# Output projections ahead of the feed-forward layers: VectorE's row chunks interleaved, five of eight squares added by accumulating DMA inside SBUF

## The reference, cut to what matters

```python
def first_block(x, ...):
    for layer in range(DEPTH):                 # DEPTH = 2
        h = _rmsnorm(x, norm_mix_g[layer])
        mix = ...                              # layer 0: gated recurrence, layer 1: stick-breaking attention;
                                               # both end in y @ w_out, 1024 x 1024
        x = x + mix
        h = _rmsnorm(x, norm_ffn_g[layer])     # x * rsqrt(mean(x*x) + eps) * g
        x = x + _swiglu(h, ffn_w_gate[layer], ffn_w_up[layer], ffn_w_down[layer])   # inner width 2816
    return _rmsnorm(x, final_g)
# a second block with three kinds of attention follows; the change leaves it alone
```

## Time and profile before

| | |
|---|---|
| median of 3 runs | 1893.66 us (1890.73 to 1895.09) |
| the profiled execution's own time | 1895.13 us |
| its span | 1893.5 us |
| TensorE busy | 1859.5 us, 98% of the span |
| VectorE busy | 1282.3 us, 68% |
| ScalarE busy | 943.5 us, 50% |
| GpSimd busy | 233.2 us, 12% |
| granted TensorE clock, mean | 0.995 |

### The profile page before, as it was taken

One profiled execution on the slowest core, in us unless ns is written; L12 is line 12 of the kernel. 1 busy time (PEld: TensorE's weight loads), 2 busy tenths in 40 slices (PEclk: granted clock), 3 DMA queues, 4 the chain that ended last, 5 costly groups with the idle time before them and its releaser, 6 DMA issues.

```text
span 1893.5 us, 30168 instructions
## 1 busy us (share of the span) xinstructions
PE 1859.5 (98%) x10662; PEld 1556.0 (82%) x10662; DVE 1282.3 (68%) x2220; ACT 943.5 (50%) x1573; POOL 233.2 (12%) x322
## 2 busy tenths in 40 slices
PE   9999899999999999999999999999999999999998
PEld 7787799889988777689988998776777887777777
DVE  7687888548756666778745876576676565656553
ACT  6477576325544444556623554355655344445442
POOL 3111011001000000011101100000002054432000
PEclk9999999999999999999999999999999999999999
DMA  7334577257432122167535742212313233323221
GB/s 252 106 101 123 139 182 180 101 135 184 133 104 78 56 66 66 56 167 194 134 132 141 195 122 86 68 45 62 95 56 92 83 95 80 90 79 91 76 97 66
DMA packets 79219, 208.64 MB, mean 110 GB/s; under 512 B 10208, under 2 KB 18528, under 8 KB 79120
## 3 DMA queue, kind: packets, MB, share of 16 engines
q1 hardware_dynamic: 60080, 174.16, 28.6%
q0 software_dynamic: 19040, 33.20, 10.2%
HBM read 203.12 MB, written 4.21 MB: 109 GB/s over the span
## 4 chain that ended last, share of the span: by engine, by line
PE 86%; DVE 6%; DMA 3%; ACT 3%; issue 2%; DVEq 0%; SPq 0%; ACTq 0%; POOL 0%
PE ps L645 16%; PE ps L647 15%; PE ps L646 15%; PE ps L731 4%; PE ps L732 4%; PE ps L733 4%; PE ps L933 3%; PE tr L899 3%; PE sc L731 3%; PE sc L733 3%; PE sc L732 3%; DMA Wr<-in_w 2%; PE sc L856 2%; PE sc L645 1%; PE sc L646 1%
## 5 line engine op out<-in xcount | busy, mean ns | idle before, releaser
L645 PE MATMUL ps<-Hl,Wh 128*128 128x512 f32 x784 | 329.2, 420 | 0.0
L1343 ACT ACTIVATE Wh<-Wr 128x1024 fp32r<-128x1024 f32 (+2 forms) x172 | 195.6, 1139 | 253.7 <-PE ps L647 228.3
L647 PE MATMUL ps<-Hh,Wh 128*128 128x512 f32 x784 | 307.6, 392 | 0.0
L646 PE MATMUL ps<-Hh,Wl 128*128 128x512 f32 x784 | 307.0, 392 | 0.0
L1907 DVE TENSOR_TENSOR Wl<-Wr,Wh 128x1024 fp32r<-128x1024 f32 (+2 forms) x172 | 231.1, 1344 | 103.0 <-ACT Wh L1343 101.6
L645 PE MATMUL ps<-Yl,Wh 128*128 128x512 f32 (+1 forms) x648 | 253.3, 391 | 11.5 <-DVE Wl L1907 5.6
L646 PE MATMUL ps<-Yh,Wl 128*128 128x512 f32 (+1 forms) x648 | 249.6, 385 | 0.0
L647 PE MATMUL ps<-Yh,Wh 128*128 128x512 f32 (+1 forms) x648 | 249.3, 385 | 0.0
L645 PEld LDWEIGHTS ps<-Hl,Wh 128*128 128x128 f32 x784 | 147.7, 188 | 40.3 <-issue 11.1
L647 PEld LDWEIGHTS ps<-Hh,Wh 128*128 128x128 f32 x784 | 147.6, 188 | 33.2
L646 PEld LDWEIGHTS ps<-Hh,Wl 128*128 128x128 f32 x784 | 148.2, 189 | 25.8 <-issue 0.5
(11 more groups left out here) (404 smaller groups left out, 4149.7 us busy)
## 6 DMA issues: line engine op xcount, KB each, us to landing
Wr<-in_w SPq DMA_DIRECT2D x162, 512.0 KB, 3.6
Wr<-in_w SPq DMA_DIRECT2D x32, 768.0 KB, 4.2
scr<-in_w SPq DMA_DIRECT2D x66, 256.0 KB, 4.6
Wr<-in_w SPq DMA_DIRECT2D x66, 256.0 KB, 4.6
scr<-in_w SPq DMA_DIRECT2D x22, 512.0 KB, 5.7
scr<-in_w POOLq DMA_DIRECT2D x44, 256.0 KB, 7.4
Wr<-in_w POOLq DMA_DIRECT2D x44, 256.0 KB, 4.2
Wr<-in_w SPq DMA_DIRECT2D x16, 640.0 KB, 3.8
```

The source lines that it names most:

```text
L645: pe.matmul(bank[:, 0:n], hi, rl[:, k, :], start=(k == 0), stop=False)
L646: pe.matmul(bank[:, 0:n], lo, rh[:, k, :], start=False, stop=False)
L647: return pe.matmul(bank[:, 0:n], hi, rh[:, k, :], start=False, stop=(k == kc - 1))
L1343: act.activation(place(Wh, slot, kc), place(Wr, slot, kc), ACT.Copy).then_inc(w_hi, 1)
```

## The change

At both places the output units get functions of their own, `rows_out`, on ScalarE and VectorE.

- **VectorE's order.** The splits of units 5, 6 and 7 move ahead: between `even_quarters` and `even_lo` of chunk 2 and chunk 4, and between `odd_quarters` and `odd_lo` of chunk 3. The subtraction for `El` (now `rest_lo`) moves behind the add of the next chunk to `X`. ScalarE's order follows.
- **The squares.** VectorE adds no squares while the units run. ScalarE's square 0 goes straight into `acc`; squares 1 to 5 go into `sq`, `rm` and are added to `acc` by five accumulating DMAs inside SBUF (256 KB each) that GpSimd issues, each waiting for its square and for the DMA before it (`sqa_in`). Squares 6 and 7 are added by VectorE (`add_last`) after the first read of the first pair. ScalarE's square m > 3 waits until DMA m - 3 has landed, since it reuses that DMA's source.
- **GpSimd's place for them** is behind third(1) and ahead of sum1(1).
- **The first pair.** The order of its weights is `A`, then `S3`. VectorE's first read into `sq` waits for all five DMAs. `mean_square` moves from ahead of the product of `A22` to behind that of `S2`, and the spreading from behind `S3` of pair 1 to behind `A11` of pair 1; the diagonal gets a place of its own in `Wh` and `Wl`. The sums and splits of pair 1 are put in another order between these.

```diff
@@ gpsimd, weight_sums
+                def add_squares(m0, m1):
+                    norm, at = ("ffn0", 0) if p0 == 0 else ("ffn1", 80)
+                    for m in range(m0, m1):
+                        pool.wait_ge(sq_ok, SQUARES[norm] + m + 1)
+                        wait(pool, sqa_in, at + 16 * (m - 1))
+                        pool.dma_start(acc[:, :], square_of[m], accum_op=ALU.add).then_inc(sqa_in, 16)
+
                 third(0, 0)
                 for h in range(pairs):
                     par = h % 2
+                    if h == 1 and name.endswith("a"):
+                        add_squares(1, 6)
                     pool.wait_ge(s1_in[par], summed(p0, h, par))
@@ names
+        square_of = [acc[:, :], sq[:, 1, :], sq[:, 0, :], rm[:, :], sq[:, 1, :], sq[:, 0, :], rt[:, :], sq[:, 1, :]]
@@ tensor, first_pair and pair
                         product("S3", "T3", delta, False, range(3, 4)).then_inc(w_used, 2)
-                        mean_square(norm, later=True)
...
                     product("S2", "T2", alpha).then_inc(w_used, 1)
+                    if ready:
+                        mean_square(ready, later=True)
...
                     product("S3", "T3", delta, True).then_inc(w_used, 1)
-                    if one and ready:
-                        spread(ready, d=1)
...
                     product("A11", "B11", alpha, True).then_inc(w_used, 1)
+                    if one and ready:
+                        spread(ready, d=2)
@@ scalar
+            def square_to(norm, m, src):
+
+                at = 80 * (norm == "ffn1")
+                if m > 3:
+                    act.wait_ge(sqa_in, at + 16 * (m - 3))
+                act.activation(square_of[m], src, ACT.Square).then_inc(sq_ok, 1)
+
+            def rows_out(name, norm, gu):
...
+                    if m % 2 == 0:
+                        both = tE[e].rearrange("p (a b) -> p a b", b=256)[:, 0:3:2, :]
+                        act.activation(both, X[:, c, :].rearrange("p (a b) -> p a b", b=256), ACT.Copy,
+                                       scale=v_col(norm, c)).then_inc(xe2_ok, 1)
+                        if m in (2, 4):
+                            split(u0 + m + 3, 1, KD)
+                        if m == 6:
+                            sum_hi(gu, 0, "A", 0, u0 + 7)
+                        else:
+                            square_to(norm, m, X[:, c, :])
+                        act.wait_ge(t1_ok, n_e + j + 1)
+                        act.activation(Hh[:, m, :], tE[e][:, 0:S], ACT.Copy).then_inc(hh_ok, 1)
@@ scalar, ffn_in, pair 0
+                    if n == 0 and norm:
+                        act.wait_ge(p2_ok, p0 + 1)
+                        act.wait_ge(w_used, b + 2)
+                        act.activation(first_of[0][:, :], ps[2][:, :], ACT.Copy).then_inc(dc_ok, 1)
+                        sum_hi(name, 1, "S3", 1, b + 2)
+                        sum_hi(name, 1, "A", 1, b + 2)
+                        act.wait_ge(w_used, b + 3)
+                        act.activation(last_of[0], ps[2][:, 0:256], ACT.Copy).then_inc(dc_ok, 1)
+                        root(norm)
...
@@ vector
+            def rows_out(name, nrm, gu):
+
+                u0, x0 = UNIT0[name], X0[name]
+                split(u0 + 3, 1, KD)
+                for m in range(KD):
+                    c = CHUNK[m]
+                    dve.wait_ge(w_used, u0 + (2 if m == 0 else m + 1))
+                    dve.tensor_tensor(X[:, c, :], X[:, c, :], ps[m if m < 4 else m % 2][:, :], ALU.add).then_inc(x_ok, 1)
+                    if m == 0:
+                        split(u0 + 4, 0, KD)
+                    if m % 2 == 0:
+                        if m:
+                            rest_lo(nrm, m - 1)
+                        even_quarters(nrm, m)
+                        if m in (2, 4):
+                            split(u0 + m + 3, 1, KD)
+                        if m == 6:
+                            sum_lo(gu, 0, "A", 0)
+                        even_lo(nrm, m)
+                        if m == 6:
+                            sum_lo(gu, 0, "S3", 0)
+                            second_sum(gu, 0, 0)
+                    else:
+                        odd_quarters(nrm, m)
+                        if m == 3:
+                            split(u0 + 6, 0, KD)
+                        odd_lo(nrm, m)
+                sum_lo(gu, 0, "A22", 0)
+                rest_lo(nrm, 7)
@@ vector, ffn_in, pair 0
+                    if n == 0 and norm:
+                        dve.wait_ge(sqa_in, 80 + 80 * (norm == "ffn1"))
                     read(sq[:, par, left], ps[par], first_of[par][:, right])
+                    if n == 0 and norm:
+                        sum_lo(name, 0, "S2", 0)
+                        add_last(norm, 6)
+                        add_last(norm, 7)
...
```

More of the change, by code:

```diff
@@ L238, in program @@
         ge_of = [ge, ht]
-        diag_h, diag_l = ([w[:, q, KD * P:MIXC * P] for q in range(2)] for w in (Wh, Wl))
+        diag_h, diag_l = ([w[:, 0, KD * P:MIXC * P], w[:, 1, KD * P:MIXC * P], w[:, 1, S:2 * S]] for w in (Wh, Wl))
         mem_col = root_col[:, 1, 6:8]
@@ L1380, in out_proj @@
                 u0, x0 = UNIT0[name], X0[name]
[L1381 to L1385 removed]
                 for m in range(KD - 2 if norm == "final2" else KD):
[L1387 removed]
+                    if not (pairs_in and m > 5):
                         split(u0 + m + 2, m % 2, kc_of(u0 + m + 2))
@@ L1922, in add_square, with add_last @@
                     dve.tensor_tensor(acc[:, 0:n], acc[:, 0:n], sq[:, m % 2, 0:n], ALU.add).then_inc(acc_ok, 1)
+            def add_last(norm, m):
+                base = SQUARES[norm]
+                dve.wait_ge(sq_ok, base + m + 1)
+                if m == 6:
+                    dve.wait_ge(sqa_in, 80 + 80 * (norm == "ffn1"))
+                else:
+                    dve.wait_ge(acc_ok, base + 7)
+                dve.tensor_tensor(acc[:, :], acc[:, :], square_of[m], ALU.add).then_inc(acc_ok, 7 if m == 6 else 1)
             def add_scaled(m):
@@ L2048, in out_proj @@
                 u0, x0, b0 = UNIT0[name], X0[name], OUT_BANK[name]
-                if name in ("rg_out", "sb_out"):
-                    split(u0 + 3, 1, KD)
                 for m in range(KD - 2 if nrm == "final2" else KD):
-                    dve.wait_ge(w_used, u0 + (2 if name in ("rg_out", "sb_out") and m == 0 else m + 1))
+                    dve.wait_ge(w_used, u0 + m + 1)
                     if name in DOWNS:
@@ L2064, in out_proj @@
                             dve.wait_ge(xf_ok, m + 1)
-                        bank = m if name in ("rg_out", "sb_out") and m < 4 else b0 + m % 2
-                        c = CHUNK[m] if name in ("rg_out", "sb_out") else m
-                        dve.tensor_tensor(X[:, c, :], X[:, c, :], ps[bank][:, :], ALU.add).then_inc(x_ok, 1)
-                    if name in ("rg_out", "sb_out") and m == 0:
-                        split(u0 + 4, 0, KD)
-                    if pairs_in and nrm and 2 < m < 6:
-                        split(u0 + m + 2, m % 2, KD)
@@ L2072, in out_proj @@
-                    if pairs_in and nrm and m % 2 == 0:
-                        even_quarters(nrm, m)
-                    if pairs_in and nrm and m % 2:
-                        odd_quarters(nrm, m)
+                        dve.tensor_tensor(X[:, m, :], X[:, m, :], ps[b0 + m % 2][:, :], ALU.add).then_inc(x_ok, 1)
                     if pairs_in and m == 6:
                         second_sum(pairs_in, 0, 0)
-                        if not nrm:
-                            sum_lo(pairs_in, 0, "S3", 0)
+                        sum_lo(pairs_in, 0, "S3", 0)
@@ L2090, in out_proj @@
-                    if pairs_in and nrm:
-                        add_square(nrm, m)
-                    elif nrm:
-                        norm_lo(nrm, m)
-                    if pairs_in and m == 6:
-                        sum_lo(pairs_in, 0, "A22", 0)
+                    if nrm:
+                        norm_lo(nrm, m)
+            def rows_out(name, nrm, gu):
+                u0, x0 = UNIT0[name], X0[name]
+                split(u0 + 3, 1, KD)
+                for m in range(KD):
+                    c = CHUNK[m]
[9 more added lines that the diff above has]
+                            split(u0 + m + 3, 1, KD)
+                        if m == 6:
+                            sum_lo(gu, 0, "A", 0)
+                        even_lo(nrm, m)
+                        if m == 6:
+                            sum_lo(gu, 0, "S3", 0)
+                            second_sum(gu, 0, 0)
+                    else:
+                        odd_quarters(nrm, m)
+                        if m == 3:
+                            split(u0 + 6, 0, KD)
+                        odd_lo(nrm, m)
+                sum_lo(gu, 0, "A22", 0)
+                rest_lo(nrm, 7)
```

99 lines of the change are left out of this document (49 added, 50 removed).

## The result

The changed kernel takes 1908.8 us (median of 4 runs, 1905.0 to 1909.7) against 1892.2 us before (4 runs in the same measurement, 1890.7 to 1895.1): slower by more than the 0.2% that can be told. The ratio over the runs is 1.0073, with a 95% interval of 1.0058 to 1.0088. That is 13.8 us; the quotient of the two medians, 1.0088 or 16.6 us, lies at the upper end of the interval. So the size of the loss is known to some 3 us. Forecast: 1908.0, range 1897 to 1920. The profiled execution took 1905.0 us, the fastest of the four; that of before was the slowest of its four. So the two spans lie 9.8 us apart where the medians lie 16.6.

The account below looks back on a forecast made before the run. TensorE, busy 98%, was taken to bound the kernel. Layer 0 +5.5, layer 1 +7.4 and clock +1.6 made 14.5 us on 1895.1, 1909.6; with the median 1.5 us under that execution, 1908, range 1897 to 1920.

Parts of the forecast that it names:

- The bound and the first stall: TensorE, busy 98%, bounds the kernel; its 2.8 us wait for unit 5's weights goes, unit 7 could start at 212.7.
- GpSimd's queue: Ahead of the adds: third(1) waits 6.2 us for `sum3`, goes out at 210.9, the first add at about 211.9.
- The first add: First DMA on `acc` takes 5.0 us, lands at 216.9; unit 7 starts at 219.5, 3.9 us later than before.
- The later adds: Each takes 4.2 us plus 0.05 wait; the fifth lands at 233.9, putting the product of `S2` at 235.1.
- The first rival: Adds inside SBUF are quick, 2.5 us each; unit 7 starts at 217.0, total 1899.4 us; chance 0.18.
- The second: Rival: adds are slow, 6.1 us each, since the queue stays full; the fifth lands at 242.6, total 1925; chance 0.12.
- The first pair's new order: `mean_square` behind `S2` adds 1.4 us up to `S4` of pair 0, which starts at 248.9; layer 0 is +5.5 us.
- Layer 1: The queue of loads is 1.9 us later against TensorE than in layer 0, so the layer loses 7.4 us.
- The clock: TensorE's long wait drops the clock to 1.2 GHz; layer 1 keeps two drops, layer 0 gets one: +1.6 us.
- The sum: Whole kernel: 5.5 + 7.4 + 1.6 = 14.5 us on 1895.1, 1909.6, less 1.5 for the median: 1908; chance 0.60.
- The later sum1(1) and third(2): GpSimd issues them some 10 us later; costed at nothing, up to 2 us more if adds take 6 us each.
- The third rival: The DMA chain is in time: first add landed by 213.0, unit 7 starts at 213.5, total 1887; chance 0.10.

Follow-up runs that it names:

- experiment 9: The changed kernel, but SyncE's loads of `raw_a` and `raw_22` of pair 1 bring only 64 columns: 1905.1 us, ratio 1.0070.
- experiment 10: The changed kernel, but the accumulating loads sum1(0) and third(1) bring 64 of 512 columns each: 1907.2 us, ratio 1.0068.
- experiment 11: The changed kernel with `raw_a` and `raw_22` of pair 1, sum1(0) and third(1) all cut to 64 columns: 1903.1 us, ratio 1.0055.
- Experiment 4: On top of experiment 2, the first pair's old order (`mean_square` ahead of `A22`, spreading behind pair 1's first product): 1885.9 us, ratio 0.9966.
- experiment 1: The changed kernel with adds 1 and 2 issued ahead of third(0) and add 3 behind it: 1891.3 us, ratio to before 0.9990.
- experiment 2: The changed kernel without DMAs on `acc`, VectorE adding all eight squares: 1888.0 us, ratio 0.9977.
- experiment 5: On top of experiment 4, the last `El` subtraction moved ahead of the last square's add: 1882.8 us, ratio 0.9945.
- experiment 3: The changed kernel with squares 4 and 5 in buffers of their own (`sum4`), so only square 7 waits for the first add: 1907.3 us, ratio 1.0073.
- experiment 6: The changed kernel with both the early adds of experiment 1 and the own buffers of experiment 3: 1890.1 us, ratio 0.9985.

## Why the prediction was right, and where it was not

**The bound and the first stall.** Right. TensorE's 2.8 us for unit 5 went in both layers, and unit 6 left TensorE ready at 209.25 (212.6 in before's time) as forecast (212.7).

**GpSimd's queue.** Right in kind and within half a microsecond. Third(1) was issued at 207.13, 210.5 in before's time, forecast 210.9. The first add followed at once, at 211.0, forecast 211.9.

**The first add.** Mis-sized: 5.0 us taken, 7.4 measured, above my upper bound of 6.1. I took it "between 4.0 and 6.1" by one row of a busy stretch, and wrote that the accumulating DMAs of before's trace took 4.0 to 6.1 us. That was misread: rows 11 themselves have a maximum of 6.7 us, and the 44 thirds of before (L551), 256 KB each, took:

```profile
DMA to landing us min/median/max: 4.2/7.4/8.7
```

The median of these is what the first add took. Experiments 9 to 11 show what it is made of, the transfers around it. Square 4 ran at 218.4 instead of 216.9 and unit 7 at 220.9 instead of 219.5: +5.3 us, not +3.9, an idle piece of 8.2 us, not 6.8; 2.4 us more of landing, 0.9 us less by the earlier issue.

**The later adds.** Mis-sized the other way: 4.25 us a link taken, 3.8 to 4.1 measured (215.59 to 219.41, 223.19 to 227.28), 3.3 to 3.6 of it landing. The fifth was issued at 227.28 and with 3.3 us is there at 230.6, 233.9 in before's time, exactly as forecast: it began later and ran faster. VectorE's read started at 230.76, and its wait is put down to ScalarE's copy, not to the chain:

```profile
230.76 0.42 DVE L2166 TENSOR_TENSOR sq<-ps,rstd 128x256 f32<-128x256 f32 x1 [1.40 <-ACT rstd L1497]
```

In layer 1 the read did wait 1.80 us for the fifth add. In neither layer did TensorE wait ahead of the product of `S2`, as the prediction had it; its short wait, 0.84 us, stood one product earlier, for ScalarE's copy. `S2` came at 232.37, 235.7 in before's time against 235.1, and `S4` at 249.2 against 248.9. Layer 0 is +5.8 there where +5.5 stood, but the 5.8 hold 1.8 us of slow clock that the forecast counted apart: errors that nearly cancel, and a total that looks better than its terms.

The rule of the Trainium skill ("DMA: Bandwidth & Descriptors", "Anatomy of one DMA — SWDGE") that I weighed against the rows gives 2.6 us as an estimate. This trace disagrees by 0.7 us for the adds in a quiet stretch (3.3) and by 4.8 us for the first one. The first rival, quick adds of 2.5 us, fell with it. The second, 6.1 us for each add, fell too: of the adds in after only the first of each layer took longer than 3.6 us.

**The first pair's new order.** Costed at 1.4 us, the length of `mean_square`, up to `S4` of pair 0, and at nothing behind it. From `S2` to that `S4` it is 13.5 us against 12.4, so about the right size, but for another reason: waits for ScalarE's copies and for `Wl`. Behind it 1.7 us more came in layer 0 and 1.9 in layer 1, a term that the forecast lacks. Experiment 4 shows where such waits come from: 2.5 us of idle time from 240 to 262 us with the new order, none with the old.

**Layer 1.** Too high up to `S4` of pair 0. Forecast +7.4; in these traces the way from unit 4 to `S4` of pair 0 is 49.3 us before and 53.9 after, +4.6. The queue was later there than in layer 0, as foreseen, but by 1.3 us (the waits of 9.46 and 8.18), not 1.9. The rest is the clock: before's lost 3.4 us in its two stretches at 1.2 GHz, and I had both stay. Both are gone from the granted clock of after, and one took their place at unit 7.

**The clock.** In kind right, in the sum wrong. Busy times by stretch, as in rows 13; the third figure from the right is the granted clock:

```profile
210.00:215.00 5.00, 0.00 (x0) 0.00 (x0) 0.00 (x0) 0.00 (x0) 0.00 (x0) 0.64 0.80 168
215.00:220.00 5.00, 2.42 (x6) 1.94 (x7) 3.72 (x7) 2.97 (x5) 1.46 (x2) 0.50 0.31 52
825.00:830.00 5.00, 4.22 (x12) 3.37 (x13) 4.56 (x9) 3.52 (x5) 0.87 (x1) 0.58 0.50 86
```

The clock falls to 0.50, 1.2 GHz, while TensorE idles. The first nine matmuls of unit 7 start every 0.43 us instead of every 0.227 (218.18, 218.60): 9 x 0.2 = 1.8 us, close to the 1.7 per stretch that I had. But layer 0 gained one and layer 1 went from two to one, so the traces differ by about nothing, where I added 1.6.

**The sum.** Up to `S4` of pair 1 the traces have 7.5 + 6.5 = 14.0 us; the forecast was 14.5. Its terms were 5.5, 7.4 and 1.6 for the clock; with the clock taken apart (1.8 us more in layer 0, 1.7 us back in layer 1) the measured ones are 5.7, 8.2 and 0.1. Up to `S4` of pair 0 alone they are 4.0 and 6.3. So the forecast was 2.6 us too high up to there and 1.5 us too high in the clock, and the 3.6 us that it lacks behind that `S4` made up for most of both. By the ratio the loss is 13.8 us and by the medians 16.6, so these runs don't decide whether 14.5 was too high or too low. That 1908.0 stands beside 1908.8 is in part luck: the base of 1893.7 was 1.5 us above the median that before had in this measurement, and without that the forecast would have been near 1906.7.

**The later sum1(1) and third(2)** cost nothing by themselves: no wait of TensorE in the second pair is put down to them. The third of pair 3, two places further in GpSimd's queue, did hold ScalarE and with it TensorE (the wait of 0.80 us at 254.08, see experiment 4). The third rival, a chain in time, was right about what it takes: experiment 1 issues the adds early enough, and the long wait goes.

## What to carry to other kernels

In these runs a DMA on an engine's queue was as late as what stood ahead of it there, and then took longer by what was in flight; look up when the queue is reached and how full it is at that moment, before its length in a quiet stretch, and take the price from the rows of all transfers of its kind, not from one. Work taken off an engine at 68% bought nothing here, while what took its place stood on the path of the one at 98%: the gain of this change lay in the new order of the output units' steps (experiments 2, 4 and 5). A changed order of the sums also moves the loads that wait for them (experiment 4). A buffer reused behind a DMA makes an engine that was never the bound carry its latency to all that follow (experiment 3 shows that a free buffer only moves the wait, if the result is needed soon anyway).

## What was unexpected of the hardware

- The packets of accumulating DMAs took 5.8 us of all 16 DMA engines per MB from 204 to 216 us, those of plain loads in the same stretch 2.8. How much of a packet's time is waiting for the other queue's the view does not tell.
- A 256 KB add inside SBUF landed 3.3 us after its issue in a quiet queue; in a full one 5.4 to 9.8 (experiments 10 and 6), whether it stood ahead of the third of pair 1 or behind it. With 32 KB instead of 256 a link of the chain shortened from 3.8 to 2.7 us.
- Two executions can stand 3.3 us apart before they reach anything that was changed (unit 4 of layer 0 at 196.26 and 192.92). So two traces are set against each other from a common instruction on.
- One idle piece of TensorE of 8.2 us cost 1.8 us more behind it in layer 0, at half the clock for nine matmuls, and behind one of 9.5 us in layer 1 eight matmuls had it (825.78 to 829.28).
